# A two-layer decoder step in five passes instead of four, with one PSUM bank per product

## What is computed

```python
# layer 0: recurrent block            # layer 1: sliding-window attention (window 128)
u  = rmsnorm(h) ; xg = u @ w_in_a     u = rmsnorm(h) ; q, k, v, gate = split(u @ w_in_b)
xb = conv4(xg[:, :1024])              s = q k^T / 8 - slope * dist   (sink column per head)
r, i = sigmoid(blockdiag(xb))         o = softmax(s) v
hl = scan(a(r), b(r, i) * xb)         h = h + (o * silu(gate)) @ w_out_b
h  = h + (hl * silu(xg[:, 1024:])) @ w_out_a
# after each layer
h = h + sigmoid(rmsnorm(h) @ w_ple_gate[i]) * (p[i] @ w_ple_proj[i])
```

## Time and profile before

| | us |
|---|---|
| median of three runs | 2128.01 (2126.4 to 2129.05) |
| the profiled execution, device time | 2127.22 |
| its span | 2125.4 |
| TensorE busy | 2025.4 (95%) |
| VectorE busy | 1166.7 (55%) |
| ScalarE busy | 904.2 (43%) |
| GpSimd busy | 618.2 (29%) |

### The profile page before, as it was taken

The page is one execution under the profiler, slowest core; times in us unless marked ns, Lnnn a source line. Parts: engine busy times, 40 slices in busy tenths (PEclk is TensorE's granted clock), DMA queues, the critical chain, the costliest instruction groups (busy, mean ns, idle before and its releaser), DMA issues.

```text
span 2125.4 us, 39197 instructions
## 1 busy us (share of the span) xinstructions
PE 2025.4 (95%) x16450; PEld 1943.2 (91%) x16450; DVE 1166.7 (55%) x2240; ACT 904.2 (43%) x1687; POOL 618.2 (29%) x468
## 2 busy tenths in 40 slices
PE   6899999889999999989999999998999999998996
PEld 6889998789999999878999999987999999997896
DVE  8874415864587331684459443277347834238633
ACT  5664434555365321463446432156235632126421
POOL 6465752355512111022212311112230231112211
PEclk9999999899999999999999999989999999999998
DMA  7566883237836555214555646511464655541243
GB/s 273 179 206 238 300 307 138 90 127 267 291 140 226 182 199 197 103 61 155 180 193 180 234 153 224 177 60 60 169 222 169 229 178 185 198 147 61 93 163 135
DMA packets 85359, 376.73 MB, mean 177 GB/s; under 512 B 10560, under 2 KB 34496, under 8 KB 49472
## 3 DMA queue, kind: packets, MB, share of 16 engines
q1 hardware_dynamic: 85184, 374.23, 49.6%
HBM read 287.28 MB, written 86.92 MB: 176 GB/s over the span
## 4 chain that ended last, share of the span: by engine, by line
PE 74%; DVE 16%; ACT 3%; POOL 3%; issue 3%; DMA 1%; SPq 0%; POOLq 0%; DVEq 0%; ACTq 0%
PE psum L1103 64%; DVE scores L924 3%; PE psum L1181 3%; DVE conv_out L828 2%; PE psum L1193 2%; PE psum L1142 2%; DVE scores L907 1%; DVE gate_tanh L868 1%; POOL w_split L484 1%; DVE row_max L896 1%; DVE lru_or_o L852 1%; POOL square_sum_in L493 1%; PE psum L1228 1%; PE psum L1229 1%; PE psum L1166 1%
## 5 line engine op out<-in xcount | busy, mean ns | idle before, releaser
L1103 PE MATMUL psum<-b_hi,w_split 128*128 128x260 f32 x4608 | 781.3, 288 | 0.4 <-POOL w_split L484 0.4
L1103 PE MATMUL psum<-a_hi,w_split 128*128 128x260 f32 x4096 | 687.7, 287 | 9.5 <-DVE conv_in L820 5.1
L1103 PEld LDWEIGHTS psum<-b_hi,w_split 128*128 128x128 f32 x4608 | 651.8, 192 | 4.2 <-issue 2.6
L1103 PEld LDWEIGHTS psum<-a_hi,w_split 128*128 128x128 f32 x4096 | 575.5, 190 | 16.2 <-issue 7.5
L1103 PE MATMUL psum<-b_lo,w_split 128*128 128x260 f32 x2304 | 469.3, 286 | 0.0
L1103 PE MATMUL psum<-a_lo,w_split 128*128 128x260 f32 x2048 | 414.6, 284 | 0.0
L1103 PEld LDWEIGHTS psum<-b_lo,w_split 128*128 128x128 f32 x2304 | 361.4, 192 | 0.0
L1103 PEld LDWEIGHTS psum<-a_lo,w_split 128*128 128x128 f32 x2048 | 318.6, 190 | 0.0
L493 POOL TENSOR_TENSOR square_sum<-square_sum,square 128x520 f32<-128x520 f32 x112 | 148.5, 1326 | 468.6 <-ACT square L604 468.6
L484 POOL TENSOR_TENSOR w_split<-w_stage,w_split 128x1024 fp32r<-128x1024 f32 x68 | 168.5, 2479 | 158.9 <-ACT w_split L597 158.7
L604 ACT ACTIVATE square<-resid 128x520 f32<-128x520 f32 x112 | 71.5, 638 | 282.4 <-DVE resid L993 196.8
(11 more groups left out here) (158 smaller groups left out, 2633.9 us busy)
## 6 DMA issues: line engine op xcount, KB each, us to landing
w_split<-kept_big SPq DMA_DIRECT2D x204, 1024.0 KB, 4.8
kept_big<-w_split SPq DMA_DIRECT2D x68, 1024.0 KB, 6.6
w_stage<-w_big SPq DMA_DIRECT2D x68, 512.0 KB, 4.9
w_split<-kept_small SPq DMA_DIRECT2D x48, 256.0 KB, 4.0
x_stage<-x SPq DMA_DIRECT2D x24, 260.0 KB, 5.2
y_out<-resid SPq DMA_DIRECT2D x3, 2080.0 KB, 11.9
resid<-x SPq DMA_DIRECT2D x3, 2080.0 KB, 10.1
p_stage<-p SPq DMA_DIRECT2D x8, 520.0 KB, 6.0
```

The lines of the kernel that those rows point to most:

```text
L1103: ins = nc.tensor.matmul(PSUM[:, 2 * p + a, 0:C], WHL[:, s, w, k, :], x[:, k, a * C:(a + 1) * C], start=(k == 0 and n == 0), stop=(k == nk ...
```

## The change

The tokens are split anew: four passes of 384 prompt tokens and two sample sequences (392 tokens), then one of 512 prompt tokens without samples. The class `Tokens` holds the sizes of each pass. Every product is now at most 512 tokens wide, so each tile's three products are one matmul each, into one bank of four that rotate (`bank`), and a big product is 24 matmuls. Attention has 12 units a pass with 4 tiles of filling in the first four passes and 16 with 3 in the last. The split weights are read back four times instead of three, into a ring of five slots: the fifth (`W5`) lies where the staging buffers of the first pass were. Prompt and samples are slices of one array now, so their loads and stores are two DMAs each. The recurrent and convolution states of all samples are loaded once at the start and stored once at the end, instead of in every pass.

```diff
-GROUPS = 4
...
-C = T // 2
...
-FLAT = TP + PAD + SG * SEG
...
+class Tokens:
+
+
+    def __init__(self, first, blocks, seq, seqs):
+        self.p0, self.nb, self.s0, self.sg = first * BLK, blocks, seq, seqs
+        self.tp, self.ts = blocks * BLK, seqs * ST
+        self.t = self.tp + self.ts
+        self.pad_at = self.tp + PAD
+        self.flat = self.pad_at + seqs * SEG if seqs else self.tp
+        self.nu = blocks * NKV
+        self.fill = (KT - 2) * KT // self.nu
+        self.whole = {max(0, -(-KT * (j - 1) // self.fill) - 1): j for j in range(1, KT)}
...
+SGD = 2
+PASSES = [Tokens(3 * i, 3, SGD * i, SGD) for i in range(4)] + [Tokens(12, 4, 0, 0)]
...
+RING_AGAIN = 5
...
-PAIR = []
-_turn = 0
-for _b in ORDER:
-    if _b[0] in "Pp" or _b == ("v", 0):
-        PAIR.append(3)
-    else:
-        PAIR.append(_turn)
-        _turn ^= 1
...
+        def bank(c, n):
+
+            return PSUM[:, c % BANKS, 0:n]
...
+        def split(g, c):
+
+
+            s = c % RING if g == 0 else ((g - 1) * NBLK + c) % RING_AGAIN
+            return W5[:] if s == RING else WHL[:, s]
...
                     return
-                s = c % RING
                 if g:
-                    before = c // RING + 1 if g > 1 or c >= RING else NBLK // RING
-                    sp.wait_ge(proj_done.sem, proj_done.at(g, c - RING + 1))
-                    sp.wait_ge(w_kept[s].sem, w_kept[s].at(0, before))
-                    sp.dma_start(split_of(c), kept_of(c)).then_inc(w_again[s].sem, 16)
+                    i = (g - 1) * NBLK + c
+                    if i < RING:
+                        sp.wait_ge(proj_done.sem, proj_done.at(0, NBLK - RING + i + 1))
+                        sp.wait_ge(w_kept[i].sem, w_kept[i].at(0, NBLK // RING))
+                    elif i == RING:
+                        sp.wait_ge(w_lo.sem, w_lo.at(0, NBLK))
+                    else:
+                        sp.wait_ge(proj_done.sem, proj_done.at(g, c - RING_AGAIN + 1))
+                    if i >= RING and g == 1:
+                        sp.wait_ge(w_kept[c % RING].sem, w_kept[c % RING].at(0, c // RING + 1))
+                    again = w_again[i % RING_AGAIN]
+                    sp.dma_start(only(c, split(g, c)), kept_of(c)).then_inc(again.sem, 16)
                     return
...
 
                     if g:
-                        pe.wait_ge(w_again[c % RING].sem, w_again[c % RING].at(g - 1, c // RING + 1))
+                        i = (g - 1) * NBLK + c
+                        again = w_again[i % RING_AGAIN]
+                        pe.wait_ge(again.sem, again.at(0, i // RING_AGAIN + 1))
                     else:
                         pe.wait_ge(w_lo.sem, w_lo.at(0, c + 1))
-                    pe.wait_ge(proj_free.sem, proj_free.at(g, before_in_pair(c) + 1))
-                s, p = c % RING, PAIR[c]
+                    if g or c >= BANKS:
+                        pe.wait_ge(proj_free.sem, proj_free.at(g, c - BANKS + 1))
+                w, t = split(g, c), PASSES[g].t
                 for k in range(k0, k1):
                     if ready is not None:
                         pe.wait_ge(ready.sem, ready.at(g, k + 1))
-                    for n, (w, x) in enumerate(((0, hi_t), (0, lo_t), (1, hi_t))):
-                        for a in range(2):
-                            ins = nc.tensor.matmul(PSUM[:, 2 * p + a, 0:C], WHL[:, s, w, k, :], x[:, k, a * C:(a + 1) * C],
-                                                   start=(k == 0 and n == 0), stop=(k == nk - 1 and n == 2))
+                    for n, (part, x) in enumerate(((0, hi_t), (0, lo_t), (1, hi_t))):
+                        ins = nc.tensor.matmul(bank(c, t), w[:, part, k, :], x[:, k, 0:t],
+                                               start=(k == 0 and n == 0), stop=(k == nk - 1 and n == 2))
...
-                    pe.wait_ge(ri_read.sem, ri_read.at(g, n))
-                hw = FLAT // 2
+                    pe.wait_ge(ri_read.sem, ri_read.at(g, n - 1))
+                f, at = PASSES[g].flat, 4 + 2 * (n % 2)
                 for w in range(2):
-                    for a in range(2):
-                        ins = nc.tensor.matmul(PSUM[:, 4 + 2 * w + a, 0:hw], WRI[:, w * KT + n, :],
-                                               XC[:, n % 2, a * hw:(a + 1) * hw], start=True, stop=True)
+                    ins = nc.tensor.matmul(PSUM[:, at + w, 0:f], WRI[:, w * KT + n, :], XC[:, n % 2, 0:f],
+                                           start=True, stop=True)
                 ins.then_inc(ri_done.sem, 1)
 
```

More of the change, by code:

```diff
@@ L34 @@
 SEQ = 2048
-GROUPS = 4
+GROUPS = 1
 TP = SEQ // GROUPS
@@ L52 @@
 BLK = 128
-NB = TP // BLK
-NU = NB * NKV
 SW = WIN + ST
+class Tokens:
[10 more added lines that the diff above has]
+PASSES = [Tokens(3 * i, 3, SGD * i, SGD) for i in range(4)] + [Tokens(12, 4, 0, 0)]
+NP = len(PASSES)
+LAST = NP - 1
+assert PASSES[-1].p0 + PASSES[-1].tp == SEQ and SGD * sum(g.sg > 0 for g in PASSES) == NSEQ
+TM = max(g.t for g in PASSES)
+TPM = max(g.tp for g in PASSES)
+FM = max(g.flat for g in PASSES)
+NBM = max(g.nb for g in PASSES)
 EPS = 1e-6
@@ L99 @@
 CONSTS = 4
-PAIR = []
-_turn = 0
-for _b in ORDER:
-    if _b[0] in "Pp" or _b == ("v", 0):
-        PAIR.append(3)
-    else:
-        PAIR.append(_turn)
-        _turn ^= 1
-def before_in_pair(c):
-    return next(p for p in range(c - 1, c - NBLK - 1, -1) if PAIR[p % NBLK] == PAIR[c])
-FREE_HEAD = 4
+BANKS = 4
+assert NBLK % BANKS == 0
 def is_small(c):
@@ L222, in build @@
[L222 to L232, removed]
+        VT = sb_at("v_t", [2, TM], F32, t_at)
@@ L286, in build @@
         consts_in = stage("consts_in", 0, step=16)
+        with_s = [int(g.sg > 0) for g in PASSES]
+        later = [int(g > 0) for g in range(NP)]
+        parts = [16 * (1 + n) for n in with_s]
+        events = [g.nu + n for g, n in zip(PASSES, with_s)]
         memset_done = stage("memset_done", 0)
@@ L408, in _ @@
             keep_weights(0)
[L410 removed]
+            for g, p in enumerate(PASSES):
                 for c in range(NBLK):
[L412 to L418 removed]
+                    if g == 0:
+                        load_weights(0, c + AHEAD)
+                        if c + 1 < NBLK:
+                            keep_weights(c + 1)
+                        if c + 1 == NBLK:
+                            load_weights(1, AHEAD)
+                    else:
+                        load_weights(g, c + RING_AGAIN - 1)
@@ L522, in _ @@
                 split_low(0, j)
-            for g in range(GROUPS):
+            for g, p in enumerate(PASSES):
                 for c in range(NBLK):
@@ L683, in _ @@
                 split_high(0, j)
-            for g in range(GROUPS):
-                chain[0] = 0
+            for g, p in enumerate(PASSES):
                 for c in range(NBLK):
@@ L1199, in sample_scores @@
                 for quad in range(NKV):
-                    for s in range(SG):
+                    for s in range(SGD):
                         for par in range(2):
```

703 lines of the change are left out of this document (380 added, 323 removed).

## The result

Of seven runs each, the kernel before took 2126.76 us in the median (2125.48 to 2130.75) and the changed one 2140.67 (2133.91 to 2147.11). The ratio is 1.0064, with a 95% interval from 1.0047 to 1.0081: slower by 0.6%, where 2066 us and a gain of 3% were forecast. The profiled execution of the changed kernel took 2143.4 us, with a span of 2141.6.

What follows compares the result with a forecast made beforehand. TensorE, busy 95% of the span, was taken as the bound, with attention held by handing units between engines. 9.2 + 441.5 + 3 x 374.3 + 471.6 + 18.1 = 2063.3 us of span, hence 2066 us; range 2035 to 2140.

Steps and rivals of the forecast that it cites:

- Matmuls: All tile products: 165.8 ns at 392 columns and 215.8 at 512, so 1660 us become 1519, 141 less.
- Rival B: Every matmul pays the 11.8 ns, 9.3 more than counted; 63 us in all, so 2129, no change; chance 0.16.
- The first pass: X and G 120.6, O to q 135, attention 105.9, o to p 80: 441.5 us against 556.0.
- 28 big blocks at 4.5: First pass, O to q: staging sets 4.5 us per big block, eight small ones at 1.1, 135 us together.
- rival D's first half: First pass held by its DMAs, 21 + 8 us more; with X and G late too, 2111 us; chance 0.14.
- D's bound of 316 GB/s: First pass, O to q and o to p: DMA moves at most 316 GB/s, needing 156 and 88 us.
- X and G of the later passes: Passes of 392: 83 us, between 78.4 and 92.9, as TensorE (74.5) and VectorE (72.2) wait for each other.
- the small slices: New loads and stores of 32 bytes a row: 0 us, at worst 25 us of VectorE waiting at O.
- the covered reading of the weights in later passes: Later passes read 1 MB in about 4.0 us, 263 GB/s, hidden with a lead of four blocks.
- Attention: Passes of 392: 22.6 us of start and 71.5 for twelve units with their filling matmuls.
- The last pass: Pass of 512: X and G 100.6, O to q 160.6, attention 25.0 and 91.2, o to p 94.2; sum 471.6 us.
- Rival C: Matmul cost goes with columns, 181 ns at 392; adds 116 us, 2182 in all, slower; chance 0.14.

Runs made afterwards that it cites:

- experiment 6: Changed kernel with the pass of 512 tokens put first and the four of 392 after it; 2100.75 us median, 0.9867 of the kernel before.
- experiment 7: Changed kernel storing only the high half of each split weight block in the first pass, read back twice later; 2126.06 us in one run.
- experiment 3: Wide-pass-first kernel with projection matmuls of its four passes of 392 cut to 320, 192, 128 and 64 columns; 2098.63 us.
- experiment 8: Changed kernel with one tap of VectorE's causal convolution left out; 2131.33 us in one run.

## Why the prediction was wrong

**The step that failed** is in *Matmuls*: "I read them as a floor near 120 ns for changing weights, which a matmul of 260 columns just misses to cover", and from it the price of 165.8 and 215.8 ns. The floor is real, but lower, near 114 ns; what 260 columns paid is a constant on top of the columns, and wider matmuls pay it too: 11.8 ns at 260, 13.5 at 320, 14.0 at 392, and 14.3 at 512 by the stage o of the last pass in the changed kernel:

```profile
2024.90:2068.60 43.70, 43.70 (x195) 36.15 (x194) 14.35 (x18) 11.85 (x19) 12.95 (x10) 1.00 0.47 168
```

(43.7/192 = 227.6 ns, the few other matmuls counted in.) The gate records were taken as nearest in length; they are plain float32, another kind of operand, and what they pay did not carry over. All the tile products now cost 6912 x 177.3 + 1728 x 227.6 = 1619 us, not 1519: of 141 us, 41 are left. In the dense stages of the later passes the excess over the forecast is this term: 720 x 11.5 ns = 8.3 us from O to q (8.1 measured), 432 x 11.5 = 5.0 from o to p (4.7). The Trainium skill's gap (TensorE: Matmul & The Clock Gate, "Back-to-back issue gap") of N/2.4 + 2.5 ns, which it gives for an isolated matmul, holds for neither width: the trace has 11.5 and 11.8 ns more.

**Rival B** is thus right in its mechanism. Its 9.3 ns were 11.5 and 11.8, and its 2129 us would then be about 2144. That this lies so near to 2140.67 is partly luck: it would put 5 us on the first pass, which took 25.8 more than forecast, and 20 on the last, which took 8.6 more.

**The first pass** was forecast at 441.5 us and took 467.3. Counted against the third pass, half of these 25.8 us is the price again (8.1 and 4.7), though where staging sets the pace the two are not parted. The rest is what staging costs beyond the same stages of the third pass: 13.4 us from O to q where 10.4 were forecast, 11.9 from o to p for 7.4, and 20.4 in attention for 11.8, while X and G came at 120.0 (120.6). "28 big blocks at 4.5" was too short: with eight small ones at 1.1 the 146.1 us leave 4.9 a block. The loads were priced at 4.9 us from the whole program, and beside the stores they take 5.7. This is rival D's first half, smaller than it was priced (20.3 us over the forecast in the two stages, where D has 29), and experiments 6 and 7 show it from both sides. D's bound of 316 GB/s is not what held it: in experiment 3 the pass of 192 columns moved 370 GB/s for 65 us. Why attention, which stages little, loses so much in the first pass was not tried; it loses 20.4 us in the changed kernel, 15 with half of the stores (106.8 against 91.8), and 10.5 with the wide pass first (121.7 against 111.2).

**X and G of the later passes**: 87.5 instead of 83, of which one tap of VectorE decides 3.8 us (experiment 8). Each waits for the other, as forecast. The price alone adds 384 x 11.5 ns = 4.4 us to TensorE's side, so the two causes overlap; how the 4.5 us over the forecast divide between them was not parted.

**Right** were the small slices at no cost (DMA packets under 512 bytes number 23936, yet stage O, which would wait for them, takes 35.6 us in the third pass, against 34.1 for o, and its one wait, 1.3 us, is for GpSimd's L539) and the covered reading of the weights in later passes. The kernel before had 10560 such packets already, so "no row here has such a piece" was a misreading. Attention, where 94.1 were 91.6, came near by luck in part: with the price as measured the forecast would have been 94.1 + 192 x 11.5 ns = 96.3, so its other terms were 4.7 us too long. The last pass took 480.2 instead of 471.6: 4.8 of it from o to p, 5.3 from O to q, 3.5 in X and G, and -5.0 in attention.

**Rival C** (cost by the columns, 181 ns) has failed by 4 ns at 392 and by 9 at 512. Its bound, that a matmul of 392 over some 175 ns decides against the change, holds for this order of the passes alone: experiment 6 is 26 us faster than the kernel before at the same 177.3.

**Open** stays what the 14 ns are. They go neither with the bank, the adding, the tiles nor the load, and 5 of them go with the format or the step of the operands.

## What to carry to other kernels

Take the price of a wider matmul from records of the same operand format, or measure it: a rest over the columns is no floor until a row at a second width shows it. Whatever is done once, in the first pass, should stand beside the longest pass: its loop of load, split and store does not shrink with the tokens, and putting the wide pass first was worth 40 us here. Before narrowing a pass, set the round trip of each staging buffer against the matmuls of a block, with the landing time of that stretch and not of the whole program.

## What was not expected of the hardware

In the sweep of widths TensorE's clock fell to 0.50, the lower level (1.2 GHz), in the pass of 128 columns, and it did not rise again while TensorE was busy without a break. Windows of that kernel: the last 4 us before the fall, two waits for GpSimd's L539 (2.15 and 2.41 us), then up to the rise, which came in attention. The last row is from the kernel with half of the weights, in its pass of 392 columns on 64 rows:

```profile
1294.00:1298.00 4.00, 3.12 (x28) 2.98 (x27) 3.69 (x7) 2.30 (x4) 1.51 (x2) 1.00 1.03 399
1298.10:1303.40 5.30, 1.01 (x4) 0.71 (x3) 0.99 (x1) 1.48 (x3) 3.52 (x6) 0.50 0.20 85
1303.40:1472.10 168.70, 168.43 (x809) 163.21 (x811) 47.63 (x88) 37.33 (x73) 24.39 (x25) 0.50 0.59 206
...
1351.20:1586.00 234.80, 234.80 (x743) 227.99 (x741) 39.54 (x65) 33.24 (x59) 24.16 (x24) 0.50 0.40 140
```

168.43 us busy of 168.70 at half clock, and 234.80 of 234.80 with half of the rows. In the changed kernel, behind the wait that ended at 913.76, the clock was back at 1.00 by 917.40. Not every stretch of narrow matmuls is slow: stage o of the pass of 128 columns, and of the pass of 192, kept the full clock, both with 22.6 us. What brings the clock back was not tried. With the floor and the clock, the kernel that streams 320, 192, 128 and 64 columns instead of 392 took 2098.63 us, 2 less than the whole work; with half of the weights it took 2238.09. Narrow tiles thus lose twice here: by the floor, and in long stretches by the clock.
